# Stick-breaking reverse sums: two rounded (fp32r) products of a high and a low part instead of one fp32 product

## The chip, the cores and the metric

The kernel runs on one core of one Trainium2 chip. The metric is the device time of one execution in microseconds (us). A profiled execution of the same program gives, beside its time, a record of what each engine did: TensorE (PE, its weight loads PEld), VectorE (DVE), ScalarE (ACT), GpSimd (POOL) and the DMA queues.

## The reference

A first block (an input product, a pooling mixer, forgetting attention, stick-breaking attention, an output product and a gated MLP) and a second block of two layers run over 256 tokens and 16 meta tokens, with a model width of 1024. All data is float32. The change lies in the stick-breaking attention of the first block, of 6 heads of width 64:

```python
z = jnp.einsum('bhqd,bhkd->bhqk', qb, k32) * scale
strict = pos[None, :] < tq[:, None]
log_beta = jax.nn.log_sigmoid(z)
log_1m = jnp.where(strict, jax.nn.log_sigmoid(-z), 0.0)
later = lax.cumsum(log_1m, axis=3, reverse=True) - log_1m
a = jnp.where(strict, jnp.exp(log_beta + later), 0.0)
return jnp.einsum('bhqk,bhkd->bhqd', a, v)
```

`log_sigmoid(-z)` is minus the softplus of z, and `log_beta + later` is z plus the sum of `log_1m` over the key itself and all later ones. The kernel computes it in that form.

## The kernel before

The whole network is one program with a hand-written instruction stream for each engine and semaphores between them. Activations lie feature by token, 128 features to a partition block. The weights come as 275 slabs of 128x1024 through a ring of four (`raw`). ACT copies each slab to a rounded part `whi` (fp32r), DVE subtracts to get `wlo` (fp32r), and PE multiplies a weight column or row by three products (`three`, L1122 to L1124): high by high, high by low, low by high. Splits run three slabs ahead of PE (`split_ahead`).

The stick-breaking stage works head by head, on scores transposed to keys by queries. 272 keys are three tiles of 128, 128 and 16 partitions. Of each tile only the queries that can see it are kept: 256, 144 and 16 columns, side by side in one PSUM bank (`SBC`, `SBN`, together `SBW` = 416). Two banks alternate (`zb`), for even and odd heads. For head i:

- PE, `sb_scores(i)` (L1275): the scores z, three products with 64 rows, into the bank. It waits until DVE has read the bank for head i-2 (`r_masked`).
- ACT, `sb_logarithm(i)` (L529 to L531): absolute value, exponential, logarithm, each over 128x416 (`z_ln`).
- DVE, `minus_softplus(i)` (L889 and L892): the softplus `sbs`, then its product with the mask of 0 and -1, `sbl` (`l_ready`). Before it overwrites `sbl` it waits for PE's sums of the head before (`r_ready`).
- PE, `sb_sums(i)` (L1316 to L1324): six fp32 products add the reverse sums to z in the bank. The stationary operand is a triangle of ones `tri` for a tile with itself, `ones` for a later tile. By tile (a, j) the columns are 256, 144, 16, 144, 16, 16 and the rows 128, 128, 16, 128, 16, 16. In the trace each fp32 product is two matmul instructions, each with its own weight load.
- DVE (L919) adds the mask `sbneg` into `sbr` (`r_masked`); ACT (L572) takes the exponential into `sbp` (`w_ready`).
- PE, `sb_values(i)` (L1333): three products with the values (`sbo_ready`).

PE's order in iteration i of the head loop is: scores of head i+1, sums of head i, values of head i-1, and in iterations 0 to 3 one row of the output product (`operand_row`, 24 fp32r matmuls of 256 columns). Iterations 4 to 6 have no such row. Behind the loop come three products with `block64` (L1350) for the head norms, and output rows 4 to 7; rows 5 to 7 need the norm factors (ACT L450, L451), DVE's L902 and the split of the operand (L460, L784).

ACT's order in iteration i is: logarithm of head i, an operand's high part (L460), a slab's high part (L414), in odd iterations from 3 the copy and the square of a finished pair (L565, L567), then the exponential of head i-1. DVE's is: softplus of head i, an operand's low part (L784), the mask add of head i-1 (L919), a slab's low part (L768).

`hidhi` and `hidlo` (128x2x256, fp32r) serve the MLPs, which run later.

Of the kernel before, what the change touches and what calls it, by code (L numbers as in the profile page):

```python
# [25 lines left out]
F32 = mybir.dt.float32  # L26
F32R = mybir.dt.float32r
ALU = mybir.AluOpType
ACT = mybir.ActivationFunctionType
AX = mybir.AxisListType.X  # L30

P = 128
# [3 lines left out]
NMETA = 16  # L36
# [92 lines left out]
SBQ = (0, 112, 240)  # L129
SBC = (0, 256, 400)  # L130
SBN = (256, 144, 16)
SBW = 416
# [10 lines left out]
def build(nc, slabs, xT, par_in, fbias_in, poolw_in, gatew_in, convw_in, out):  # L143
    with ExitStack() as ctx:
        def sb(name, shape, dt=F32):
            return ctx.enter_context(nc.sbuf_tensor(name, shape, dt))

        def sem(name):
            return ctx.enter_context(nc.semaphore(name))
# [27 lines left out]
        hidhi = sb("hidhi", [P, 2, SEQ], F32R)  # L177
        hidlo = sb("hidlo", [P, 2, SEQ], F32R)
# [4 lines left out]
        ones = sb("ones", [P, P])  # L183
        block64 = sb("block64", [P, P])
        tri = sb("tri", [P, P])
# [28 lines left out]
        def first_only(parts, *dims):  # L214
            n = 1
            for d in dims:
                n *= d
            v = shared[0:parts, place[0]:place[0] + n]
            place[0] += n
            return v if len(dims) == 1 else v.rearrange("p (a b) -> p a b", a=dims[0])  # L220
# [7 lines left out]
        sbs, sbl, sbr, sbp = first_only(P, SBW), first_only(P, SBW), first_only(P, SBW), first_only(P, SBW)  # L228
        lam = sb("lam", [P, 4, KC])

        raw_loaded = [sem(f"raw_loaded{s}") for s in range(R)]
        hi_done, lo_done, slab_used = sem("hi_done"), sem("lo_done"), sem("slab_used")
        gemm_evac, acc_ready, prod_ready = sem("gemm_evac"), sem("acc_ready"), sem("prod_ready")
# [2 lines left out]
        consts, gprod = sem("consts"), sem("gprod")  # L236
# [8 lines left out]
        p_normed, pT, pT_copied, o_ready = sem("p_normed"), sem("pT"), sem("pT_copied"), sem("o_ready")  # L245
        o_copied = sem("o_copied")
        z_ready, z_ln, l_ready, r_ready = sem("z_ready"), sem("z_ln"), sem("l_ready"), sem("r_ready")
        r_masked, w_ready, sbo_ready, sbo_copied = sem("r_masked"), sem("w_ready"), sem("sbo_ready"), sem("sbo_copied")
        pool_d, pool_mixed = sem("pool_d"), sem("pool_mixed")
        hsq, hstat, hstd = sem("hsq"), sem("hstat"), sem("hstd")  # L250
# [17 lines left out]
        consts_done = 16  # L268
# [127 lines left out]
        def _(act):  # L396
# [12 lines left out]
            def split(n, q=0):  # L409

                act.wait_ge(raw_loaded[n % R], 16 * (n // R + 1 + q))
                if n >= R:
                    act.wait_ge(slab_used, n + R * q - R + 1)
                act.activation(whi[:, n % R, :, :], raw[:, n % R, :, :], ACT.Copy).then_inc(hi_done, 1)  # L414

            def split_ahead(n, q=0):

                if n not in EARLY and n + LOOKAHEAD < NSLABS:
                    split(n + LOOKAHEAD, q)
# [37 lines left out]
            def operand_hi(s, f, k):  # L457

                act.wait_ge(af_ready, KC * f + k + 1)
                act.activation(ahi[:, k, NMETA:], af[:, k, :], ACT.Copy).then_inc(ahi_ready, 1)  # L460

            def values(g, m, dst, src):

                act.wait_ge(vT, g + 1)
                act.activation(dst, src[0:m, 0:dst.shape[1]], ACT.Copy).then_inc(v_ready, 1)
# [40 lines left out]
            for n in range(IN1, IN1 + FOX_READY):  # L506
                split_ahead(n)
                if n == IN1 + 2:
# [2 lines left out]
                    link(act.activation(lf[:, 2, :], lf[:, 1, :], ACT.Exp, scale=-1.0))  # L511
                    act.activation(lf[:, 3, :], lf[:, 2, :], ACT.Ln, bias=1.0).then_inc(fl_ln, 1)
            split_ahead(IN1 + FOX_READY)
            for g in range(3):
                m = (P, P, NMETA)[g]
                values(g, m, vtok[0:m, g, 0:FOX_W], acc_bank[2 + g % 2])

            zb = (stat_bank, aux_bank)
# [36 lines left out]
            for i in range(SB_HEADS + 2):  # L555
                if 1 <= i < SB_HEADS:
                    sb_logarithm(i)
                if i < 5:
                    operand_hi(A_MIX1, F_MIX1, i)
                    if i:  # L560
                        split_ahead(OUT1 + i - 1)
                if i >= 3 and i % 2:
                    pair = (i - 3) // 2
                    act.wait_ge(sbo_ready, 2 * pair + 2)
                    act.activation(y[:, 5 + pair, :], gemm_bank[0][:, 0:SEQ], ACT.Copy).then_inc(sbo_copied, 1)  # L565
                    act.wait_ge(sbo_copied, pair + 1)
                    act.activation(sq[:, 3 + pair, NMETA:], y[:, 5 + pair, :], ACT.Square).then_inc(hsq, 1)  # L567
                if 1 <= i <= SB_HEADS:
                    act.wait_ge(r_masked, i)
                    if i >= 2:  # L570
                        act.wait_ge(sbo_ready, i - 1)
                    act.activation(sbp[:, :], sbr[:, :], ACT.Exp).then_inc(w_ready, 1)  # L572
# [49 lines left out]
            for u in range(MOBA_U + 3):  # L622
# [15 lines left out]
                if 2 <= u <= 2 * CONV_C and u % 2 == 0:  # L638
                    i = u // 2 - 1
# [9 lines left out]
                if u == MOBA_U:  # L649
                    for k in range(CONV_C):  # L650
                        g, b = COL["ab_ln_g_2"] + k, COL["ab_ln_b_2"] + k
# [60 lines left out]
            for i in range(2 * KC):  # L712
                if IN3 + i < OUT3 - 1:
                    split_ahead(IN3 + i)
                if i < KC:
                    w, b = COL["c_conv_w_2"] + KC * (LRU_T - 1) + i, COL["c_conv_b_2"] + i
# [9 lines left out]
                if i in (12, 13):  # L726
                    j = 4 * (i - 12)
# [28 lines left out]
        def _(dve):  # L756
# [113 lines left out]
            for u in range(FOX_U + 1):  # L870
# [5 lines left out]
                if u == 6:  # L876

                    dve.wait_ge(pool_d, 1)
                    for w, buf, p0, c in ((2, win, 0, 0), (4, win2, HD, 0), (8, win, 0, 1), (16, win2, HD, 1)):
                        ins = dve.scalar_tensor_tensor(pd[p0:p0 + HD, c, :], buf[p0:p0 + HD, c, NMETA:], 1.0 / w,  # L880
                                                       proj[p0:p0 + HD, PU + c, NMETA:], ALU.mult, ALU.subtract)
                    ins.then_inc(pool_d, 1)

            zb = (stat_bank, aux_bank)

            def minus_softplus(i):

                dve.wait_ge(z_ln, i + 1)
                link(dve.scalar_tensor_tensor(sbs[:, :], zb[i % 2][:, 0:SBW], 0.0, sba[:, 2, :], ALU.max, ALU.add))  # L889
                if i >= 1:  # L890
                    dve.wait_ge(r_ready, i)
                dve.tensor_tensor(sbl[:, :], sbs[:, :], sbm[:, :], ALU.mult).then_inc(l_ready, 1)  # L892


# [15 lines left out]
            for i in range(SB_HEADS + 1):  # L910
                if 1 <= i < SB_HEADS:
                    minus_softplus(i)
                if i < 5:
                    operand_lo(A_MIX1, i)
                if i >= 1:
                    dve.wait_ge(r_ready, i)
                    if i >= 2:
                        dve.wait_ge(w_ready, i - 1)
                    dve.tensor_tensor(sbr[:, :], zb[(i - 1) % 2][:, 0:SBW], sbneg[:, :], ALU.add).then_inc(r_masked, 1)  # L919
                if 1 <= i < 5:  # L920
                    split_ahead(OUT1 + i - 1)
            split_ahead(OUT1 + 4)
# [66 lines left out]
            for u in range(MOBA_U + 3):  # L989

                softmax_step(u, MOBA_U, FOX_U, MOBA_N, alibi_bias)
                if u in IN2_STEP:
                    c = IN2_STEP[u]
# [52 lines left out]
            c = COL["c_lambda_2"]  # L1046
# [23 lines left out]
            for i, c in enumerate(IN3_ORDER):  # L1070
                take(IN3 + i, col_bank(i), c, ahead=IN3 + i < OUT3 - 1)
                if 1 <= i <= KC:
# [3 lines left out]
                    for t in range(LRU_T - 1):  # L1076
                        w = COL["c_conv_w_2"] + KC * t + k
                        x0 = NMETA - LRU_T + 1 + t
                        ins = dve.scalar_tensor_tensor(af[:, k, :], proj[:, 8 + k, x0:x0 + SEQ], par[:, w:w + 1],
                                                       af[:, k, :], ALU.mult, ALU.add)  # L1080
# [27 lines left out]
            for k in range(FINAL_D):  # L1108
                g = GAIN[N_FINAL] + k
                ins = dve.tensor_scalar(af[:, k, :], h[:, k, NMETA:], par[:, g:g + 1], None, ALU.mult)  # L1110
# [7 lines left out]
        def _(pe):  # L1118
# [137 lines left out]
            for t in range(2):  # L1256
                ins = pe.transpose(aux_bank[:, FOX_HEADS * t:FOX_HEADS * t + FOX_HEADS],
                                   cum[:, NMETA + P * t:NMETA + P * t + P], ident[0:FOX_HEADS, 0:FOX_HEADS])
# [7 lines left out]
            zb = (stat_bank, aux_bank)  # L1266
# [18 lines left out]
            for u in range(FOX_U + 3):  # L1285
# [6 lines left out]
                if u == FOX_U - 1:  # L1292
# [4 lines left out]
                    for g in range(4):  # L1297
                        b, c = HD * (g % 2), g // 2
                        ins = pe.matmul(gemm_bank[1][b:b + HD, SEQ * c:SEQ * c + SEQ], poolw[b:b + HD, c, :],
                                        pd[b:b + HD, c, :], start=True, stop=True)  # L1300
# [13 lines left out]


            def sb_sums(i):  # L1316
                pe.wait_ge(l_ready, i + 1)
                for a in range(3):
                    for j in range(a, 3):
                        m = P if j < 2 else NMETA  # L1320
                        c = SBC[a] + SBQ[j] - SBQ[a]
                        ins = pe.matmul(zb[i % 2][:, c:c + SBN[j]], (tri if a == j else ones)[0:m, :],  # L1322
                                        sbl[0:m, SBC[j]:SBC[j] + SBN[j]], start=False, stop=False, skip_group_check=True)
                ins.then_inc(r_ready, 1)  # L1324

            def sb_values(i):
# [73 lines left out]
            for u in range(MOBA_U + 3):  # L1400
# [5 lines left out]
                if new_pair:  # L1406
                    pe.wait_ge(gemm_evac, taken)
                    for g in range(2):
                        ins = pe.transpose(acc_bank[2][:, P * g:P * g + P],
                                           proj[:, 16 + u // 4, NMETA + P * g:NMETA + P * g + P], ident[:, :])  # L1410
# [11 lines left out]
                if u == LN_MEAN_STEP:  # L1422
                    pe.wait_ge(conv, CONV_C)
                    for k in range(CONV_C):
                        ins = pe.matmul(half(acc_bank[3], 0), ones[:, :], cv[:, k, :], start=(k == 0), stop=(k == CONV_C - 1))
                    ins.then_inc(ln_mean, 1)
                if u == LN_VAR_STEP:
                    pe.wait_ge(ln_sq, CONV_C)
                    for k in range(CONV_C):
                        ins = pe.matmul(half(acc_bank[3], 1), ones[:, :], sq[:, k, NMETA:], start=(k == 0),  # L1430
                                        stop=(k == CONV_C - 1))
# [27 lines left out]
            for i in range(2, 2 * KC):  # L1459
# [4 lines left out]
                if k < KC:  # L1464
# [5 lines left out]
                    for g in range(2):  # L1470
                        ins = pe.matmul(half(acc_bank[k % 4], g), gatew[:, g, k, :], af[:, k, :], start=True, stop=True)  # L1471
# [79 lines left out]
```

## Time and profile before

| | us |
|---|---|
| median of 3 runs | 976.01 (lowest 975.49, highest 4328.1) |
| profiled execution, its own time | 977.4 |
| its span, first to last instruction | 975.7 |
| PE busy in the span | 937.5 |
| DVE busy | 601.3 |
| ACT busy | 467.5 |
| mean granted TensorE clock | 0.983 |

Shares of the span say which engine is full over the whole program. What a stage is worth is read in the stage: the stick-breaking heads lie between 119 and 161 us of the span. Start times in the timeline are us from the span's start. The chain of work that ended last leads back from the end to what released each piece.

### The profile page before, as it was taken

What the parts mean: (1) busy time and instruction counts of PE and PEld (TensorE: products, weight loads), DVE (VectorE), ACT (ScalarE), POOL (GpSimd) and SP (SyncE); (2) the same over time, 40 slices, a digit from 0 to 9 for tenths busy, and PEclk for the clock granted to TensorE, in tenths of its full rate; (3) what the DMA queues carried; (4) which work ended last, traced back from release to release, by engine and by line L of the source; (5) the groups of instructions that cost most, each with busy time, mean ns of one, the idle gap of its engine ahead of it and who ended that gap; (6) DMA issues with size and microseconds to landing.
All of it is one profiled execution on the core that took longest, in us unless ns stands there. A gap on an engine that the chain in (4) does not pass through costs nothing.

```text
span 975.7 us, 19747 instructions
## 1 busy us (share of the span) xinstructions
PE 937.5 (96%) x7466; PEld 887.3 (91%) x7466; DVE 601.3 (62%) x976; ACT 467.5 (48%) x741; POOL 91.0 (9%) x152
## 2 busy tenths in 40 slices
PE   8999899999999998999899999999898999999996
PEld 8977687899999998877789999999898999999995
DVE  4655434755666667645566665665887876656655
ACT  5344545644444446433464444444668554434442
POOL 5110000200000003920010000000122010000001
PEclk9999989999999999999899999999998999999998
DMA  7432121566655554732255556655444545555541
GB/s 245 151 109 90 62 65 61 200 194 194 190 180 184 182 183 127 235 109 66 87 173 174 192 174 193 191 174 194 139 143 150 173 140 186 186 192 181 181 163 43
DMA packets 44007, 152.57 MB, mean 156 GB/s; under 512 B 5692, under 2 KB 5948, under 8 KB 43964
## 3 DMA queue, kind: packets, MB, share of 16 engines
q1 hardware_dynamic: 40752, 146.36, 46.3%
q0 software_dynamic: 2912, 5.48, 1.8%
q8 instruction: 30, 0.49, 0.2%
q10 hardware_dynamic: 300, 0.14, 0.1%
q14 instruction: 13, 0.11, 0.0%
HBM read 148.58 MB, written 1.05 MB: 153 GB/s over the span
## 4 chain that ended last, share of the span: by engine, by line
PE 87%; DVE 6%; ACT 3%; issue 1%; DMA 1%; SPq 0%; DVEq 0%; ACTq 0%
PE bank L1122 25%; PE bank L1124 24%; PE bank L1123 24%; DVE alo L791 2%; PE bank L1231 2%; PE bank L1395 2%; PE bank L1322 2%; PE bank L1209 1%; DVE h L801 1%; PE bank L1191 1%; ACT whi L414 1%; DVE wlo L768 1%; PE bank L1151 1%; PE bank L1220 1%; PE bank L1471 1%
## 5 line engine op out<-in xcount | busy, mean ns | idle before, releaser
L1122 PE MATMUL bank<-ahi,whi 128*128 128x256 f32 (+1 forms) x1416 | 408.5, 289 | 10.1 <-DVE alo L784 4.9
L1124 PE MATMUL bank<-ahi,wlo 128*128 128x256 f32 (+1 forms) x1416 | 401.7, 284 | 0.0
L1123 PE MATMUL bank<-alo,whi 128*128 128x256 f32 (+1 forms) x1416 | 401.2, 283 | 0.0
L768 DVE TENSOR_TENSOR wlo<-raw,whi 128x1024 fp32r<-128x1024 f32 x275 | 337.7, 1236 | 40.5 <-ACT whi L414 40.2
L414 ACT ACTIVATE whi<-raw 128x1024 fp32r<-128x1024 f32 x275 | 284.5, 1051 | 133.9 <-PE bank L1124 124.4
L1122 PEld LDWEIGHTS bank<-ahi,whi 128*128 128x128 f32 x1416 | 270.3, 191 | 15.6 <-issue 7.1
L1123 PEld LDWEIGHTS bank<-alo,whi 128*128 128x128 f32 x1416 | 270.5, 191 | 0.4
L1124 PEld LDWEIGHTS bank<-ahi,wlo 128*128 128x128 f32 x1416 | 270.5, 191 | 0.0
L1122 PE MATMUL bank<-hidhi,whi 128*128 128x256 f32 x688 | 192.6, 280 | 0.0
L1124 PE MATMUL bank<-hidhi,wlo 128*128 128x256 f32 x688 | 192.4, 280 | 0.0
L1123 PE MATMUL bank<-hidlo,whi 128*128 128x256 f32 x688 | 192.4, 280 | 0.0
L1123 PEld LDWEIGHTS bank<-hidlo,whi 128*128 128x128 f32 x688 | 129.5, 188 | 0.0
L1122 PEld LDWEIGHTS bank<-hidhi,whi 128*128 128x128 f32 x688 | 129.4, 188 | 0.0
L1124 PEld LDWEIGHTS bank<-hidhi,wlo 128*128 128x128 f32 x688 | 129.3, 188 | 0.0
L1021 DVE SCALAR_TENSOR_TENSOR hid<-bank,rstd 128x256 f32<-128x256 f32 x64 | 27.1, 424 | 126.4 <-PE bank L1124 124.4
L677 ACT ACTIVATE hidhi<-hid 128x256 fp32r<-128x256 f32 x64 | 26.9, 420 | 137.1 <-DVE hid L1021 133.9
L810 DVE SCALAR_TENSOR_TENSOR proj<-bank,rstd 128x256 f32<-128x256 f32 (+1 forms) x56 | 23.9, 429 | 55.1 <-PE bank L1124 52.7
L320 POOL TENSOR_TENSOR sq<-sq 128x256 f32<-128x256 f32 (+1 forms) x20 | 19.7, 1012 | 362.5 <-ACT sq L442 362.5
L592 ACT ACTIVATE hidhi<-hid 128x256 fp32r<-128x256 f32 x22 | 9.2, 418 | 61.9 <-DVE hid L945 61.9
L1144 PE MATMUL bank<-ahi,whi 128*128 128x256 f32 (+1 forms) x96 | 24.7, 296 | 7.3 <-ACT ahi L435 4.5
L373 POOL DMA_DIRECT2D shared<-zpad x64 | 31.5, 501 | 1.4 <-POOL zpad L368 1.2
L1028 DVE TENSOR_TENSOR hidlo<-hid,hidhi 128x256 fp32r<-128x256 f32 x64 | 27.2, 425 | 3.5 <-ACT hidhi L677 1.1
(181 smaller groups left out, 761.7 us busy)
## 6 DMA issues: line engine op xcount, KB each, us to landing
raw<-in_slabs SPq DMA_DIRECT2D x275, 512.0 KB, 3.5
shared<-zpad POOLq DMA_DIRECT2D x64, 35.5 KB, 3.0
shared<-in_convw POOLq DMA_DIRECT2D x4, 512.0 KB, 6.2
h<-in_xT SPq DMA_DIRECT2D x4, 272.0 KB, 3.8
vtok<-in_gatew POOLq DMA_DIRECT2D x2, 512.0 KB, 4.7
out<-y SPq DMA_DIRECT2D x4, 256.0 KB, 2.2
par<-in_par ACTq DMA_DIRECT2D x1, 72.0 KB, 3.2
poolw<-in_poolw ACTq DMA_DIRECT2D x1, 64.0 KB
```

The source lines that it names most:

```text
L320: pool.tensor_tensor(t8[:, j, :] if i == N_MIX0 else a, a, b, ALU.add).then_inc(sum_ready, 1)
L373: pool.dma_start(zsh[32 * s:32 * s + 32, k, g, :], zpad[32 * g:32 * g + 32, k, s:s + CONV_X])\
L414: act.activation(whi[:, n % R, :, :], raw[:, n % R, :, :], ACT.Copy).then_inc(hi_done, 1)
L677: act.activation(hidhi[:, f % 2, :], hid[:, f % 2, :], ACT.Square).then_inc(hid_hi, 1)
L768: dve.tensor_tensor(wlo[:, n % R, :, :], raw[:, n % R, :, :], whi[:, n % R, :, :].bitcast(F32), ALU.subtract).then_inc(lo_done, 1)
L810: dve.scalar_tensor_tensor(proj[:, d, lo:], src[:, lo:T1], scale, rstd[:, lo:], ALU.mult, ALU.mult).then_inc(gemm_evac, 1)
L1021: dve.scalar_tensor_tensor(hid[:, f % 2, :], col_bank(f)[:, NMETA:T1], 0.0, rstd[:, NMETA:], ALU.max, ALU.mult).then_inc(gemm_evac, 1)
L1028: dve.tensor_tensor(hidlo[:, f % 2, :], hid2[:, f % 2, :], hidhi[:, f % 2, :].bitcast(F32), ALU.subtract).then_inc(hid_lo, 1)
L1122: pe.matmul(dst, hi, xh, start=start, stop=False, skip_group_check=True)
L1123: pe.matmul(dst, hi, xl, start=False, stop=False, skip_group_check=True)
L1124: return pe.matmul(dst, lo, xh, start=False, stop=stop, skip_group_check=True)
L1144: pe.matmul(dst, w[:, slot, k, :], ahi[:, k, lo:], start=(k == 0 and w is whi), stop=False, skip_group_check=True)
```

## The change

The masked negative softplus `sbl` is no longer the operand of the sums. ACT copies it, rounded, into `sbhi`; DVE subtracts to get `sblo`, rounded too. Both are views of `hidhi` and `hidlo`. Rounded copies `tri_r` and `ones_r` are made once by ACT, before the values of the forgetting attention. PE does the six products with `sbhi` and then the six with `sblo`: 12 fp32r matmuls where there were 6 fp32 products. PE waits for `sb_lo` instead of `l_ready`. DVE overwrites `sbl` when its own subtraction has read it. ACT's copy waits for `l_ready` and for PE's sums of the head before; it stands in ACT's order behind the slab split and ahead of the pair's copy and the exponential of head i-1. DVE's subtraction stands behind the mask add of head i-1 and ahead of the slab split.

```diff
+        sbhi, sblo = (t[:, :, :].rearrange("p a b -> p (a b)")[:, 0:SBW] for t in (hidhi, hidlo))
+        tri_r, ones_r = sb("tri_r", [P, P], F32R), sb("ones_r", [P, P], F32R)
...
+        sb_hi, sb_lo, sb_ones = sem("sb_hi"), sem("sb_lo"), sem("sb_ones")
...
             split_ahead(IN1 + FOX_READY)
+            act.wait_ge(consts, consts_done)
+            act.activation(tri_r[:, :], tri[:, :], ACT.Copy).then_inc(sb_ones, 1)
+            act.activation(ones_r[:, :], ones[:, :], ACT.Copy).then_inc(sb_ones, 1)
...
                     if i:
                         split_ahead(OUT1 + i - 1)
+                if i < SB_HEADS:
+                    act.wait_ge(l_ready, i + 1)
+                    if i >= 1:
+                        act.wait_ge(r_ready, i)
+                    act.activation(sbhi[:, :], sbl[:, :], ACT.Copy).then_inc(sb_hi, 1)
...
                 if i >= 1:
-                    dve.wait_ge(r_ready, i)
+                    dve.wait_ge(sb_lo, i)
                 dve.tensor_tensor(sbl[:, :], sbs[:, :], sbm[:, :], ALU.mult).then_inc(l_ready, 1)
...
                     dve.tensor_tensor(sbr[:, :], zb[(i - 1) % 2][:, 0:SBW], sbneg[:, :], ALU.add).then_inc(r_masked, 1)
+                if i < SB_HEADS:
+                    dve.wait_ge(sb_hi, i + 1)
+                    dve.tensor_tensor(sblo[:, :], sbl[:, :], sbhi[:, :].bitcast(F32), ALU.subtract).then_inc(sb_lo, 1)
...
             def sb_sums(i):
-                pe.wait_ge(l_ready, i + 1)
-                for a in range(3):
-                    for j in range(a, 3):
-                        m = P if j < 2 else NMETA
-                        c = SBC[a] + SBQ[j] - SBQ[a]
-                        ins = pe.matmul(zb[i % 2][:, c:c + SBN[j]], (tri if a == j else ones)[0:m, :],
-                                        sbl[0:m, SBC[j]:SBC[j] + SBN[j]], start=False, stop=False, skip_group_check=True)
+                pe.wait_ge(sb_ones, 2)
+                pe.wait_ge(sb_lo, i + 1)
+                for part in (sbhi, sblo):
+                    for a in range(3):
+                        for j in range(a, 3):
+                            m = P if j < 2 else NMETA
+                            c = SBC[a] + SBQ[j] - SBQ[a]
+                            ins = pe.matmul(zb[i % 2][:, c:c + SBN[j]], (tri_r if a == j else ones_r)[0:m, :],
+                                            part[0:m, SBC[j]:SBC[j] + SBN[j]], start=False, stop=False, skip_group_check=True)
                 ins.then_inc(r_ready, 1)
```

## Rows read from the trace of the kernel before

**Rows 1.** The page: span, busy time by engine, and the chain by engine.

```profile
span 975.7 us, 19747 instructions
...
PE 937.5 (96%) x7466; PEld 887.3 (91%) x7466; DVE 601.3 (62%) x976; ACT 467.5 (48%) x741; POOL 91.0 (9%) x152
...
PE 87%; DVE 6%; ACT 3%; issue 1%; DMA 1%; SPq 0%; DVEq 0%; ACTq 0%
```

**Rows 2.** Chain that ended last, 118 to 168 us: start, length, engine and line.

```profile
119.91 3.91 PE bank L1322 x12
...
127.10 0.21 PE bank L1124
...
129.24 1.33 PE bank L1275 x6
...
151.24 1.00 PE bank L1275 x6
152.24 2.18 PE bank L1322 x12
...
155.45 2.18 PE bank L1322 x12
157.63 1.05 PE bank L1333 x6
158.76 0.56 ACT shared L572
159.36 1.12 PE bank L1333 x6
```

**Rows 3.** Timeline of PE, head 4's sums: start, us, engine, line, operation.

```profile
152.16 0.70 PE L1322 MATMUL bank<-shared,tri 128*128 128x256 f32 x2
152.70 0.73 PE L1322 MATMUL bank<-shared,ones 128*128 128x144 f32 x4
...
153.04 0.39 PE L1322 MATMUL bank<-shared,ones 16*128 16x16 f32 x2
...
153.36 0.51 PE L1322 MATMUL bank<-shared,tri 128*128 128x144 f32 x2
153.80 0.39 PE L1322 MATMUL bank<-shared,ones 16*128 16x16 f32 x2
...
154.34 0.43 PE L1333 MATMUL bank<-shared,vtok 128*64 128x256 f32 x1
```

**Rows 4.** Timelines of fp32r products: nine from 181.63, and loads, one then two.

```profile
181.63 1.32 PE L1151 MATMUL bank<-alo,whi 128*128 128x256 f32 x9 [0.49 <-DVE alo L791]
...
181.63 0.19 PEld L1151 LDWEIGHTS bank<-alo,whi 128*128 128x128 f32 x1 [0.69 <-DVE alo L791]
...
181.63 0.30 PEld L1151 LDWEIGHTS bank<-alo,whi 128*128 128x128 f32 x2 [0.69 <-DVE alo L791]
```

**Rows 5.** Timelines of ACT and DVE: what stands around the added copy and subtraction.

```profile
118.56 0.40 ACT L460 ACTIVATE ahi<-af 128x256 fp32r<-128x256 f32 x1
...
119.88 0.42 DVE L784 TENSOR_TENSOR alo<-af,ahi 128x256 fp32r<-128x256 f32 x1
...
154.61 0.59 DVE L892 TENSOR_TENSOR shared<-shared 128x416 f32<-128x416 f32 x1
155.12 0.58 DVE L919 TENSOR_TENSOR shared<-bank,shared 128x416 f32<-128x416 f32 x1
```

**Rows 6.** Windows: busy us of PE, PEld, DVE, ACT, POOL; granted clock; DMA.

```profile
116.20:119.60 3.40, 0.98 (x7) 0.78 (x6) 2.10 (x5) 2.69 (x6) 0.00 (x0) 1.00 0.00 0
119.60:129.90 10.30, 10.30 (x41) 9.13 (x41) 3.85 (x7) 3.42 (x6) 0.00 (x0) 0.50 0.15 51
...
467.80:471.20 3.40, 2.19 (x12) 1.11 (x11) 2.80 (x8) 0.90 (x5) 0.00 (x0) 1.00 0.39 129
471.20:478.00 6.80, 5.92 (x26) 5.69 (x26) 3.46 (x8) 2.83 (x8) 0.00 (x0) 0.50 0.26 88
```

## The prediction

> **What bounds the kernel now.** I read the page first, for the engine that is full, and then the chain that ended last, for what sets the end in the stage that the change touches. TensorE (PE) is busy in 96% of the span and makes up 87% of the chain [rows 1]. What lengthens or shortens PE's own sequence therefore comes out at the end one for one, unless it falls into a wait. In the chain of the stage, the six sums of the heads (line L1322, each 12 matmul records) stand with all their length: 3.91 us for head 0 and 2.18 us for each later one [rows 2]. That is 3.91 + 5 x 2.18 = 14.8 us, 1.5% of the kernel, so no price of these sums can move it by much more. From head 4's scores to head 5's values the chain leaves PE only for ACT's last exponential at 158.76, with a gap of 0.7 us between two value products [rows 2].
>
> The four windows show the third thing that matters, the granted clock of PE. It is 1.00 (2.4 GHz) for most of the kernel. It fell to 0.50 (1.2 GHz) at 119.6, behind a stretch in which PE was busy 0.98 of 3.4 us, and came back at 129.9, when PE had been in dense fp32r rows for 6 us. It fell again at 471.2, behind 2.19 busy of 3.4 us, for 6.8 us [rows 6]. Head 0's 3.91 us against 2.18 is that clock, a factor of 1.79 [rows 2].
>
> **Why 12 passes cost 2.18 us.** The starts in the timeline [rows 3] cut the sums of head 4 into pieces: 0.54 us for two passes of 256 columns, 0.34 for two of 144, 0.32 for two of 16 rows, 0.44 for two of 144, 0.54 for four of 16 rows, sum 2.18. Three numbers reproduce all five. A weight load takes 0.11. An fp32 pass of 256 columns takes 0.22 and one of 144 takes 0.12, and the next load hides under it. At each change between 128 and 16 rows PE first empties (0.09), and then the next load is bare. So 128-row tiles: 0.11 + 2 x 0.22 + 2 x 0.12 + 0.09 = 0.88; 16 rows: 2 x 0.11 + 0.01 + 0.09 = 0.32; 0.11 + 2 x 0.12 + 0.09 = 0.44; 4 x 0.11 + 0.01 + 0.09 = 0.54. The streaming of columns is about 1.0 us of the 2.18; the rest is loads and emptying, and the change does not touch those kindly.
>
> The Trainium skill states the emptying as a rule (TensorEngine Tiling (Array Packing), Key Properties: a change of the tiling mode drains the engine), and the trace agrees: 0.09 us at each change of rows.
>
> **The change part by part.**
>
> *The sums.* There are still 12 matmuls and 12 loads. An fp32r matmul of 256 columns takes half an fp32 pass: nine of them from 181.63 take about 0.12 each. But the second fp32r load begins 0.11 after the first, as in fp32 [rows 4]. So I take load 0.11, 256 columns 0.11, 144 columns 0.06, 16 columns 0.01, emptying 0.09. One part (high or low): (0.11 + 0.11 + 0.06 + 0.09) + (0.11 + 0.01 + 0.09) + (0.11 + 0.06 + 0.09) + (0.11 + 0.11 + 0.01 + 0.09) = 0.37 + 0.21 + 0.26 + 0.32 = 1.16. Two parts: 2.32 us against 2.18. The streaming falls by half, but the sequence 128, 16, 128, 16 rows is now walked twice and its emptying and bare loads double. So each head costs +0.14 us, and at the low clock 4.16 for 3.91, +0.25.
> No row shows an fp32r product of under 256 columns, so I bound it. Below: no emptying and only loads back to back, 12 x 0.11 plus entry and end, 1.5 us. Above: narrow products stream no faster than both fp32 passes together (144 columns in 0.24, not 0.06), 0.4 more for each part, 3.1 us. I take 2.32, because both its loads and its emptying stand in rows.
>
> *The copy and the subtraction.* The nearest rows are 0.40 and 0.42 for 256 columns to fp32r, and 0.56 (ACT) and 0.59 (DVE) for 416 columns [rows 2, 5]; I take 0.55 for ACT and 0.6 for DVE. For heads 1 to 4 they are hidden: PE is in values (1.0), a row (24 x 0.12 = 2.9) and the next scores (1.0), 4.9 us, while they run. Without that cover they cost 1.15 us a head. Two heads lack it.
> Head 0: ACT is free behind its operand copy at about 118.9, and the copy ends at 119.4. DVE subtracts behind L784 (119.88) [rows 5], from 120.2 to 120.8. The sums began at 119.9 [rows 2]; now they start at 120.8, and with the semaphore's way I take +1.0, and +0.25 for their own length, row 0 starts 1.25 later. The clock comes back at the same 129.9, so 0.35 of it is made good, since head 1's scores now run at the full clock (1.33 us in the trace, 1.00 otherwise [rows 2]). Heads 1 to 3 add 3 x 0.14. Head 5's scores end 1.3 later, at 153.5.
> Head 5: from its scores to `sbl` the trace has 152.24 to 155.2 [rows 2, 5], 2.96 us. Copy and subtraction make that about 4.2, so its sums start at 157.7 instead of 155.4: +2.3, with PE idle for 0.85 us behind the values of head 3. DVE's mask add of head 4 stands ahead of the subtraction, but runs beside ACT's copy. Own length +0.14: +2.4. Everything behind waits on this chain: values of head 4, the last exponential, values of head 5, the norms, rows 5 to 7.
>
> *The rest is hidden.* The copies of `tri` and `ones` come while ACT waits for PE's transposes of the values. The subtraction pushes DVE's slab split back 0.6 us; slabs are split three ahead. ACT's copy ahead of the exponential of head i-1 has the same cover. `sbl` is free earlier, which takes away DVE's wait in head 1, off the path. No DMA is added.
>
> Sum without the clock: +2.4 us.
>
> *The clock.* In the tail of the stage, heads 4 and 5, PE would have sums that stream columns for 0.5 of 2.3 us, 1.0 us of values, a gap of 0.85, the same sums again, and the known gap of 0.7. Before, the sums streamed for 1.0 of 2.2 us and there was no first gap. The stretches ahead of the two falls [rows 6] were of that sort: short products with gaps. I judge a fall in this tail more likely than not. Price, if it falls at about 157: head 5's sums 4.16 for 2.32 and the values of head 4 1.9 for 1.0 are +2.7, for a stretch of 6.8 us; for one of 10.3 us the values of head 5 and the norms add another 1.5. So it costs 2.7 to 4.2, I take 3.6: together +6.0.
>
> **The rivals.**
> A. The forecast: sums at 2.3 us, the two bare latencies, one fall in the tail. +6.0. For it: rows 4 for the loads, rows 3 for the emptying. Against: no row of before shows fp32r between gaps.
> B. The same without a fall: +2.4, 978.4. The clock held through the tail of before.
> C. Cheap sums (1.5 us, one end of the bound): no emptying for fp32r, or faster loads. Head 0 -0.2, heads 1 to 3 -0.68 each, so -2.2 at head 5's scores; the longer chain gives 1.1 back; -0.68: -1.8, 974.2, and with a fall about 978. It ends on the other side. It decides from sums under about 1.9 us, where the savings of five heads equal the latencies. Against it are the five pieces of rows 3. The Trainium skill (TensorE: Matmul & The Clock Gate, Weight-path perf modes) says that fast weight load is on with 128 weights and a type other than FP32. If fp32r counted as such, loads would be near a quarter, and by that rule the sums would come to about 1.5 us. The trace disagrees: fp32r loads of 128 weights lie 0.11 apart.
> D. Narrow fp32r products as slow as fp32: 3.1 us a head. Head 0 +2.6, heads 1 to 3 +0.9 each, less 0.35; head 5 chain and sums +2.0: about +7, 983. PE streams more then, so the clock likely holds.
> E. Falls in heads 1 to 3 too. Each makes a row 24 x 0.09 = 2.2 us longer (0.21 a matmul at the low clock [rows 2] for 0.12) and the values 0.9: +3. With the one in the tail +9, 985. For 2% it would take 19.5 us, more than five falls.
>
> **How the numbers follow.** A 0.45, B 0.22, C 0.13, D 0.10, E 0.10. Against the profiled execution's own 977.4 (span 975.7) the likeliest is 983.4. That execution lies 1.4 above the median of 976.0, so on the median I forecast 982.0. The range runs from C with a fall or the lower edge of B, 976.8, to E, 985.5. A change of 2%, about what a measurement of this kernel can tell from no change, is 19.5 us; the stage's sums are 14.8. Faster by over 2%: 0.005. Within 2%: 0.985. Slower by over 2%: 0.01.
>
> **What would show it.** In the profile after: L1334 or near it, 12 fp32r matmuls a head, from first start to the values' start 2.3 us (C: 1.5, D: 3.1); the starts of 16-row products 0.2 apart from their neighbours; PE idle about 1 us before head 0's sums and before head 5's, released by the subtraction; a window of clock 0.50 near 157 to 167 (A), none (B), or further ones between 130 and 150 (E). The forecast is wrong if the sums are shorter than 1.9 us, or if the granted clock before head 1 comes back at another time than 129.9.

## The result, and the profile after

The changed kernel takes 986.9 us (median of four executions, 985.75 to 990.92) beside 976.3 before. The ratio is 1.0118, interval 1.0081 to 1.0156; it is one of means, 987.6 to 976.0, and leaves out one execution of the kernel before that took 4328 us. The change is slower by 1.2%, and the time lies above my range (976.8 to 985.5). Measured again, the same kernel gave 983.8 beside 975.4, ratio 1.0088 (1.0065 to 1.0111), and that median lies inside the range. The direction and most prices held, the number of clock falls did not.

The page of the profiled execution (990.9 us, span 989.2) already shows where. In the row of the granted clock, 40 slices of about 25 us, the sixth and the seventh slice read 6, where before had 8 and 9; two slices later in the kernel that read 8 before (the 20th and the 31st) now read 9.

```profile
span 989.2 us, 19772 instructions
...
PE 949.9 (96%) x7466; PEld 897.0 (91%) x7466; DVE 604.4 (61%) x982; ACT 471.4 (48%) x749; POOL 91.0 (9%) x152
...
PEclk9999966999999999999999999999999999999998
```

The windows of the stage, cut where the clock changed (columns as in [rows 6]):

```profile
119.60:129.90 10.30, 9.30 (x40) 8.60 (x38) 5.11 (x10) 3.97 (x7) 0.00 (x0) 0.50 0.14 47
129.90:133.30 3.40, 3.40 (x20) 2.80 (x19) 0.41 (x1) 2.06 (x5) 0.00 (x0) 1.00 0.03 11
133.30:140.10 6.80, 6.80 (x30) 5.96 (x30) 3.24 (x6) 1.91 (x3) 0.00 (x0) 0.50 0.25 80
140.10:143.50 3.40, 3.40 (x21) 2.79 (x19) 0.23 (x1) 1.88 (x5) 0.00 (x0) 1.00 0.00 0
143.50:150.40 6.90, 6.90 (x30) 6.06 (x30) 3.43 (x6) 2.79 (x6) 0.00 (x0) 0.51 0.23 77
150.40:153.80 3.40, 3.40 (x21) 2.86 (x19) 0.13 (x1) 1.78 (x4) 0.00 (x0) 1.00 0.00 0
153.80:160.60 6.80, 6.80 (x29) 5.88 (x29) 3.53 (x6) 2.19 (x4) 0.00 (x0) 0.50 0.24 77
160.60:164.00 3.40, 3.40 (x22) 2.87 (x20) 0.00 (x0) 1.61 (x3) 0.00 (x0) 1.00 0.00 0
164.00:177.70 13.70, 13.00 (x41) 9.17 (x41) 3.69 (x6) 4.10 (x9) 0.00 (x0) 0.50 0.01 2
```

Head 0's low stretch is where it was [rows 6]. New are four more: behind the sums of heads 1, 2 and 3, and one of 13.7 us over heads 4 and 5. In each of the first three, the values of one head and most of a row of the output product run at 1.2 GHz. PE's busy share says nothing of it: it is 100% on both sides of each of these three falls. The chain shows the prices (start, length, engine and line; L1290 scores, L1339 sums, L1350 values):

```profile
120.37 0.51 DVE hidlo L934
121.02 3.80 PE bank L1339 x12
...
130.14 1.00 PE bank L1290 x6
131.14 2.35 PE bank L1339 x12
133.49 1.84 PE bank L1350 x6
...
140.52 1.00 PE bank L1290 x6
141.52 2.49 PE bank L1339 x12
144.01 1.85 PE bank L1350 x6
...
162.29 2.67 PE bank L1339 x12
164.96 1.85 PE bank L1350 x6
166.81 3.76 PE bank L1339 x12
...
177.88 0.70 ACT sq L454
```

The last line is the start of the norm factors. In the chain of before it stands at:

```profile
162.28 0.59 ACT sq L450
```

From the sums of head 1 to those of head 2 it is 10.4 us (131.14 to 141.52), where before needed 7.2 a head (PE does head 2's scores ahead of head 1's sums, so these begin at 129.24 + 1.33, and head 4's sums begin at 152.24, three heads later [rows 2]). Of these 3.2 us more, the sums take 0.2 (2.35 where the clock holds). The rest is values and row at the low clock.

### The profile page after: what moved, and what is told of

It is laid out like the page before. It is cut to its first block, busy times and chain, and to the rows that moved or that the text cites. A ratio compares the mean times of both kernels' runs of the same rounds, so it can differ in the third digit from the quotient of the medians.

```text
span 989.2 us, 19772 instructions
## 1 busy us (share of the span) xinstructions
PE 949.9 (96%) x7466; PEld 897.0 (91%) x7466; DVE 604.4 (61%) x982; ACT 471.4 (48%) x749; POOL 91.0 (9%) x152
## 4 chain that ended last, share of the span: by engine, by line
PE 88%; DVE 6%; ACT 3%; issue 1%; DMA 1%; SPq 0%; DVEq 0%; ACTq 0%
PE bank L1137 25%; PE bank L1139 24%; PE bank L1138 24%; DVE alo L803 2%; PE bank L1339 2%; PE bank L1246 2%; PE bank L1412 2%; PE bank L1224 1%; DVE h L813 1%; PE bank L1350 1%; PE bank L1206 1%; DVE wlo L780 1%; ACT whi L418 1%; PE bank L1166 1%; PE bank L1235 1%
## 5 line engine op out<-in xcount | busy, mean ns | idle before, releaser
L1137 PE MATMUL bank<-ahi,whi 128*128 128x256 f32 (+1 forms) x1416 | 410.8, 290 | 10.1 <-DVE alo L796 4.9
L324 POOL TENSOR_TENSOR sq<-sq 128x256 f32<-128x256 f32 (+1 forms) x20 | 19.6, 1012 | 377.1 <-ACT sq L446 377.1
```

What stands on the lines that cost most here:

```text
L1137: pe.matmul(dst, hi, xh, start=start, stop=False, skip_group_check=True)
```

## The experiments

Three theories stood against each other. **Path**: the waits ahead of heads 0 and 5 and the slightly longer sums are the loss. **Clock**: the sums in fp32r leave PE so little streaming between its rows that the clock falls, and that is most of it. **Layout**: what makes the sums thin is the change between 128 and 16 rows, and could be avoided.

Each execution gives its span and its mean granted clock, and I call (1 - clock) x span the lost clock. It is not all paid: it counts the kernel's last 6 us, in which PE does nothing, and the waits that fall into a low stretch. Over the 57 executions of the kernel before, one microsecond more of lost clock goes with 0.7 us more time (a straight line through them, worked out from the record), so I count a difference in lost clock as worth 0.7 to 1 times its size. Executions of one kernel differ, and the profiles show low stretches of different number, length and place; the kernel before itself ran from 972.6 to 980.0 at clocks of 0.988 to 0.981. So the table has means over the executions. The ratios are against the kernel before measured beside each (975.6 to 976.0 us; its lost clock was 13.4 to 14.7, and for the first line only the profile's 16.6 is known).

| kernel | executions | mean us | ratio, interval | lost clock, us |
|---|---|---|---|---|
| changed kernel, first time | 4 | 987.6 | 1.0118 (1.0081 to 1.0156) | 25.4 |
| changed kernel, again | 4 | 984.3 | 1.0088 (1.0065 to 1.0111) | 20.6 |
| copy and subtraction, fp32 sums | 8 | 983.1 | 1.0088 (1.0065 to 1.0112) | 20.6 |
| the same, again | 4 | 981.4 | 1.0061 (1.0039 to 1.0082) | 17.9 |
| fp32r products alone | 4 | 980.6 | 1.0063 (1.0038 to 1.0088) | 22.0 |
| changed kernel, two waits | 7 | 983.1 | 1.0079 (1.0053 to 1.0106) | 22.4 |
| changed, ten dense products a head | 4 | 982.6 | 1.0082 (1.0059 to 1.0105) | 13.2 |
| changed, ten thin products a head | 4 | 997.7 | 1.0231 (1.0194 to 1.0267) | 31.9 |
| changed, 128 rows throughout | 10 | 976.9 | 1.0012 (0.9992 to 1.0032) | 18.5 |
| the same, two waits | 10 | 974.8 | 0.9994 (0.9980 to 1.0008) | 17.2 |
| before, 128 rows throughout | 10 | 971.9 | 0.9957 (0.9935 to 0.9978) | 13.2 |
| the same, again | 10 | 972.9 | 0.9977 (0.9962 to 0.9992) | 13.4 |
| the same, wait of head 1 filled | 9 | 970.8 | 0.9948 (0.9930 to 0.9966) | 11.9 |

**The changed kernel again.** No edit.

> The changed kernel unaltered, measured beside those below. Lost clock (1 minus the mean granted clock, times the span) was 21 to 30 us in its first four executions and 11 to 19 in 23 of the kernel before. Clock theory: again 10 to 11 us more than before, of which the lost clock explains 8 to 10. If the clock of the first profile was a chance of that visit, it is 980 to 982.

It came to 8.6 us over before in the mean, with 7.2 us more lost clock, less than the 10 to 11 us that I expected by the clock theory, and more than the 4 to 6 if the first time was a chance (980 to 982). The first four executions lost 23.6 to 30.7 us, these 19.6 to 23.6: the first time was at the high end, but the loss is no chance of it. The profile of this execution has low stretches behind two of the heads with rows, of 3.4 us each at 135 and 152, and one of 10.2 us in the tail. So between these two profiles the number of heads hit differs, and the length of the stretches.

**One half: the copy and the subtraction, with fp32 sums.**

```diff
-                for part in (sbhi, sblo):
+                for part in (sbl,):
...
-                            ins = pe.matmul(zb[i % 2][:, c:c + SBN[j]], (tri_r if a == j else ones_r)[0:m, :],
+                            ins = pe.matmul(zb[i % 2][:, c:c + SBN[j]], (tri if a == j else ones)[0:m, :],
```

(and DVE waits for `r_ready` ahead of `sbl` again).

> The changed kernel with its copy, its subtraction and its waits, but the sums are the six fp32 products of before (2.18 us a head). The parts sbhi and sblo are computed and not used. Clock theory (the fp32r sums make TensorE's clock fall behind each head, and that is most of the 10 us): no fall in heads 1 to 4, only the two bare latencies are left, +1.0 us at head 0 and about +1.2 at head 5, so 978 to 979. Latency theory (the copy and the subtraction, waited for, are most of it): 984 or more.

> The copy and the subtraction in place with fp32 sums, a second visit: its first gave 977 to 980 in two executions and 984 to 986 in six, with a lost clock of 15 and 21 to 24 us. The lost clock of the kernel before is 11 to 19. If the two waits make the clock fall behind head 0 and in the tail, the median stays over 980 and the profile shows the low stretches at 122 to 130 and 160 to 168. If the six were a chance: 978 to 979.

Neither pure theory: medians of 984.1 and 981.0, more than the path's 978 to 979, and the second is under 984. The sums of heads 1 to 3 keep 2.18 us and the clock holds there in both profiles. In the tail the wait is as computed, and the clock falls behind it, for 6.8 us from 160.5 (the first of the two profiles; the second is alike):

```profile
152.78 1.01 PE bank L1290 x6
153.81 0.53 ACT shared L536
154.36 0.56 ACT shared L537
154.94 0.56 ACT shared L538
155.53 0.60 DVE shared L901
156.15 0.60 DVE shared L904
156.78 0.56 ACT hidhi L573
157.36 0.60 DVE hidlo L934
158.10 2.22 PE bank L1339 x12
160.32 1.50 PE bank L1350 x6
161.90 0.56 ACT shared L584
162.51 1.91 PE bank L1350 x6
```

From the end of head 5's scores (153.79) it is 4.3 us to its sums, over the logarithm, the softplus, the copy and the subtraction; I had computed 4.2. The values at the end take 1.91 instead of 1.12 [rows 2]. So the waits cost twice, once on the path and once by the clock. In the mean over the executions it is 4 to 6 us of lost clock on top of before's 14 to 15. The profiled execution shown here is one of the two short ones (979.8, lost clock 14.7); where the six long ones lost their 21 to 24 us, no profile shows.

**The other half: fp32r products alone.** DVE writes the masked softplus rounded; there is no copy, no subtraction.

```diff
-                dve.tensor_tensor(sbl[:, :], sbs[:, :], sbm[:, :], ALU.mult).then_inc(l_ready, 1)
+                dve.tensor_tensor(sbhi[:, :], sbs[:, :], sbm[:, :], ALU.mult).then_inc(l_ready, 1)
...
+                for part in (sbhi, sbhi):
```

(and both PE's sums and DVE's next product wait as before, for `l_ready` and `r_ready`).

> The other half alone. VectorE writes the masked softplus rounded to fp32r at once; the twelve fp32r products of the change run on it, the same part twice. There is no copy, no subtraction, no new wait. It leaves out the low part and adds the high one twice. Clock theory: the clock falls to 0.50 behind heads 1 to 5 as in the changed kernel, sums 2.35 us at the full clock, no wait ahead of head 0; 982 to 985. Latency theory: 977, since only 0.17 us a head is added.

980.6 in the mean, 4.9 over before, between the two expectations and nearer to the clock's. The lost clock is 7.3 us higher. In its profile the clock falls, beside head 0's stretch, in the tail only (155.6 to 165.8), not behind each head, so the part of my expectation that named heads 1 to 5 was wrong for that execution. The chain of its tail (L1331 the sums, L1342 the values) has no wait in it, and head 5's sums run at the low clock:

```profile
152.31 2.32 PE bank L1331 x12
154.63 1.03 PE bank L1342 x6
155.67 3.76 PE bank L1331 x12
```

So in the tail either half is enough: the wait with fp32 sums, or fp32r sums without a wait. Before, with neither, the clock held there [rows 2]. Each half of the change alone costs about 5 to 7 us, and both together 9 to 12.

**Dense and thin filler.** The strongest test of the clock adds work. Ten products that nobody uses, into an empty bank, ahead of the sums:

```diff
+                pe.wait_ge(sb_hi, i + 1)
+                for _ in range(10):
+                    pe.matmul(gemm_bank[1][:, 0:SEQ], tri_r[:, :], sbhi[:, 0:SEQ], start=True, stop=True, skip_group_check=True)
                 pe.wait_ge(sb_lo, i + 1)
```

and in the second kernel the same with 16 columns instead of 256 (`0:16` in place of `0:SEQ`).

> The changed kernel with ten needless fp32r products of 128x256 into an unused bank ahead of each head's sums, once the copy is there: 1.1 us of dense work a head, that fills the wait for the subtraction too. Clock theory: the clock stays at 1.00 behind heads 1 to 4, and in spite of 6 x 1.1 us of useless work the time is no longer than the changed kernel's, 982 to 987. Rival (the clock doesn't care, or the ten products don't change it): the changed kernel plus 5 to 7 us, 991 to 994.

> As the filler, but its ten needless products have 16 columns instead of 256: the same number of instructions and loads, the same 1.1 us a head, the same wait filled, almost no columns streamed. If the filler helped because it fills the wait or moves the stage in time: the filler's result, 981 to 984. If it helped because dense products keep the clock: lost clock as in the changed kernel or more (over 20 us), and 6 us of useless work on top, 989 to 994.

With the dense ones the clock stays at 1.00 through the whole stage, even behind head 0, and the kernel is no longer than without them (982.6 beside 984.3, a difference within the spread of four executions each), in spite of 6 x 1.4 us of useless work. Not all of that work is added to the path: it covers the waits of heads 0 and 5, about 1 us each, and the sums behind it take 2.13 us instead of 2.33. With the thin ones, which take 1.2 us a head where the clock is full, the lost clock is 31.9 us where the changed kernel had 20.6 and 25.4, and the kernel takes 13 us more, 997.7, which is more than the 989 to 994 I had expected. The windows of the stage, dense first:

```profile
119.00:180.00 61.00, 56.80 (x391) 50.50 (x392) 28.44 (x46) 31.52 (x58) 0.00 (x0) 1.00 0.18 58
```

```profile
119.00:180.00 61.00, 59.47 (x292) 51.35 (x292) 20.44 (x34) 21.94 (x42) 0.00 (x0) 0.69 0.11 35
```

PE reads busier in the second (59.5 us of 61) and does a quarter less (292 matmuls for 391). And the chain of each, dense and then thin (L1335 the filler, L1342 the sums, L1353 the values):

```profile
129.95 1.40 PE bank L1335 x10
131.34 2.13 PE bank L1342 x12
133.47 1.03 PE bank L1353 x6
...
138.54 1.38 PE bank L1335 x10
139.92 2.13 PE bank L1342 x12
142.05 1.03 PE bank L1353 x6
```

```profile
132.68 1.21 PE bank L1335 x10
133.89 2.69 PE bank L1342 x12
136.58 1.85 PE bank L1353 x6
```

Both kernels have the same number of instructions and loads and the same waits, and fill the same gap. Only the number of columns differs. So it is neither the delay nor the filled wait, but the streaming, that keeps or loses the clock here. That the clock causes most of the change's loss follows from the sizes: of the 8.6 us measured the second time, 7.2 us of lost clock are worth 5 to 7.

**Two waits instead of one.** PE starts the high part when the copy is there:

```diff
-                pe.wait_ge(sb_lo, i + 1)
-                for part in (sbhi, sblo):
+                for part, landed in ((sbhi, sb_hi), (sblo, sb_lo)):
+                    pe.wait_ge(landed, i + 1)
```

> The changed kernel with two waits instead of one: TensorE starts the high part's products as soon as the copy is there and waits for the subtraction only ahead of the low part's. It takes 0.6 us from the wait ahead of heads 0 and 5 and adds nothing. Path alone: -1.0 us against the changed kernel. If the gaps, too, make the clock fall: -2 to -5 us. If the gaps are nothing: no change.

983.1 against 984.3: 1.2 us in the mean, what the path alone gives, but the executions (980.3 to 987.3) spread too far to tell this from no change. The lost clock is not lower.

Its profile has no fall behind heads 1 to 3; its low stretches in the stage are head 0's (124 to 131) and one of 10 us in the tail. That makes five profiles of fp32r sums with changes of rows and no dense filler: behind or in heads 1 to 3 the clock fell three times in the first, twice in the second, three times with the thin filler, and never with the products alone or with two waits. In the tail it fell in all five. In the eight profiles with fp32 sums or with full rows (below) it never fell at heads 1 to 3. What decides whether such a head is hit in a given execution, no run shows.

**128 rows throughout.** The third tile's rows above 16 are masked to zero, so they may be multiplied.

```diff
-                            m = P if j < 2 else NMETA
+                            m = P
```

> The changed kernel with all 128 rows in every product of the sums, so that TensorE never changes between 128 and 16 rows (the rows above 16 of the third tile are masked to zero). Theory that the emptying and the bare loads make both the length and the clock's fall: sums 1.3 to 1.5 us a head instead of 2.35, no fall behind heads 1 to 3, 975 to 978. Rival, that fp32r sums are too thin however they are laid out: sums 1.5 us, but the clock still falls behind each head, 981 to 985.

> Both cures of the fp32r sums: 128 rows in all products and two waits. The changed kernel with full rows alone took 1.45 us a head and lay 0.1% above before. Expected -1.0 us from it by the path, so level with before, 974 to 976; it would beat before only if the clock gained too. The fp32 kernel with full rows (971.6 beside 975.8) should stay ahead of it.

The sums fall to 1.45 us a head, by the chain of this kernel:

```profile
129.64 1.00 PE bank L1290 x6
130.63 1.45 PE bank L1339 x12
132.09 1.03 PE bank L1350 x6
```

The kernel comes to 976.9, level with before; with two waits, 974.8. Heads 1 to 3 keep their clock in both profiles; the tail does not (155 to 163 in each), and the lost clock of the kernels stays at 17 to 19 us. The layout theory is right for the length. For the clock the fair pair is the two kernels with two waits, measured together: 17.2 us lost with full rows and 22.4 without, and the ranges of their executions do not meet (14.6 to 18.5, 18.6 to 26.6). That the gain in clock lies at heads 1 to 3 is likely but not shown, since the profile of the two waits without full rows keeps the clock there too.

**The same edit on the kernel before, and a filled wait.**

> The kernel before with the same edit alone: 128 rows in all six fp32 products of the sums. By the pieces of the kernel before (load 0.11, 256 columns 0.22, 144 columns 0.12, emptying 0.09) the sums take 1.8 us instead of 2.18, and the four bare loads and emptyings go. Theory: -0.4 us for each of six heads, more at the low clock of head 0, 973 to 974. Rival (sixteen rows cost nothing extra): 976.

> The kernel before with full rows, again, beside the filled one: 971 to 972, 4 us under before.

> The kernel before with 128 rows in all products of its sums, and ten needless fp32 products of 128x128 where TensorE waits 2.4 us for the norm factors ahead of head 1's scores. Clock theory: the clock no longer falls at 119.6, head 0's sums take 1.7 us instead of 3.1 and row 0 3 us instead of 5: 3 to 4 us below the kernel with full rows alone, 967 to 969. Rival (the fall comes anyway): no change against it, 971 to 972.

One changed line in the kernel before makes its fp32 sums 1.69 us instead of 2.18 and the kernel 3.8 and 2.8 us faster, measured twice: both intervals lie under 1. I had computed 1.8 for these sums, and neither time hit what I expected (971.9 for 973 to 974, then 972.9 for 971 to 972). The third kernel adds ten fp32 products of 128 columns while PE waits for the norm factors:

```diff
             pe.wait_ge(v_ready, 6)
+            for _ in range(10):
+                pe.matmul(acc_bank[0][:, 0:P], ones[:, :], tri[:, :], start=True, stop=True)
             pe.wait_ge(hstd, 2)
```

```profile
119.78 1.07 PE bank L1275 x6
120.85 1.69 PE bank L1322 x12
...
125.47 1.00 PE bank L1275 x6
126.47 1.69 PE bank L1322 x12
```

The fall ahead of head 0's sums is gone: 1.69 us for them, and 5.6 us to the next head's instead of 10.7 [rows 2]. Not all of that is the filler's: with full rows alone the two profiles have 8.8 and 7.2 us there. The kernel takes 970.8, 2.1 less in the mean than the unfilled one beside it, where I expected 3 to 4 and 967 to 969 in all. It is the fastest of all, 0.5% under before.

## Why the prediction was wrong, point by point

- *What bounds the kernel, and that sums cannot move it by much more than their own 14.8 us.* Right for the sums. But as a bound on the change it misled me: what the sums do to the clock is paid by the rows behind them, which are not in the 14.8. (PE does the scores of head i+1 ahead of the sums of head i. So the scores that I called head 1's, at 129.24, are head 2's, and those that I called head 4's, at 151.24, are head 5's; no number changes.)
- *Sums at 2.32 us a head.* Measured 2.35 and, the second time, 2.32 and 2.33 where the clock is full. That an fp32r product halves the streaming but keeps its load, and that the emptying is walked twice, was the right model. The upper bound (narrow products as slow as fp32) and rival D, 3.1 us, fall with it. Rival C's 1.5 us was the right length once the row changes are gone, not before: with full rows the fp32r sums take 1.45 us and the fp32 sums 1.69. I took the emptying for the change of tiling mode of which the Trainium skill speaks (TensorEngine Tiling (Array Packing), Key Properties); the runs show what a change of rows costs, but not that it is such a change. By the Trainium skill's rule on fast weight load (TensorE: Matmul & The Clock Gate, Weight-path perf modes), taken to include fp32r, I estimated 1.5 us for the sums as they stand; the trace disagrees, with 2.35. My estimate was too generous to the rule, too: the fourfold gain in that section is for fp8, and its table has none for fp32. At the low clock I had 4.16 and the trace has 3.80: I had scaled the whole length by 1.79, and it grew from 2.33 by 1.63.
- *Copy 0.55, subtraction 0.6, bare at heads 0 and 5.* Right. The profile after has PE idle 1.00 us behind the subtraction at head 0, and the half-change and the changed kernel's second profile have 4.3 us from scores to sums at head 5 for my 4.2. The other heads hid them. In the first profile head 5 hid them as well: at the low clock PE came to these sums late and did not wait.
- *The sum without the clock, +2.4 us.* Borne out as far as it can be separated: the second time's 8.6 us more, less the 5.0 to 7.2 us that the lost clock is worth, leaves 1.4 to 3.6.
- *One fall in the tail, 3.6 us.* This is the step that failed: the sum had this one fall and nothing for falls behind heads 1 to 3. The tail itself was priced nearly right. By the end of head 5's scores I had the kernel 1.3 us late, and the first profile has it 10.1 us late (162.29 for 152.24); from there to the norm factors I had 4.7 us more, and it has 5.5. I named the mechanism, put a price of 3 us on each further fall, and it measured 3.0 (10.4 less 7.2 less 0.2). But I gave several falls 0.10, since "before, the sums streamed for 1.0 of 2.2 us" seemed to set the tail apart from heads 1 to 3 by its gaps. In the first profile every head fell; in the second two of three did, for 3.4 us at a price of about 1.5 us each (8.9 us from the sums of head 1 to those of head 2). The low stretch in the tail lasted 13.7 us and then 10.2, where I had 6.8 to 10.3. What I left out was to ask of each head what I had asked of the tail: between two dense rows stand scores, sums and values, 4.4 us of short products, and the change took half the streaming from the middle of it.
- *The clock comes back at 129.9.* It did in the first profile, but that was luck: in the second it came back at 131.9, and head 0's low stretch lasted 10.3 us in some profiles and 6.8 in others (123.1 to 129.9 in the half-change).
- *The times as they came.* In the first profile the norm factors behind the heads start 15.6 us late (177.88 for 162.28). The end is 13.5 us late. About 2 us come back further on; the page shows two low slices fewer there than before, and no run separates what these are worth.
- *The range.* Its upper end stood at two new falls, the tail's and one more (985, with a margin to 985.5). The first four executions (985.75 to 990.92) lie above it, the next four (983.35 to 986.09) about it. Its other half, that the loss stays well under 2%, held.

## What to carry to other kernels

Before making a product cheaper in columns, look at what PE streams between its dense stretches: halving it saves nothing if loads and row changes set the length (2.18 us became 2.35 here), and it can cost the clock for the next dense stretch and for the products on the way there: 3.0 us behind each of three heads, of the 13.5 by which the first profile was longer. A busy share near 100% does not show this; the granted clock cut by windows does. Where a short tile of few rows stands between full ones, and its other rows can be zero, give it all 128: one line made both kernels faster, and the fp32 kernel stayed ahead.

## What the runs showed that I had not expected

- Sixty useless fp32r products of 256 columns (8.3 us of PE time) did not make the changed kernel longer; sixty of 16 columns made it 13 us slower.
- Changing between 128 and 16 rows cost more than a third of the fp32r sums: 2.35 us with it, 1.45 without; in fp32, 2.18 and 1.69.
- One and the same kernel ran from 972.6 to 980.0 us in 23 executions, and the mean granted clock went with it, 0.988 to 0.981 at the two ends. A change of half a per cent needs many executions here.
